# Two more of the 22 gated up-projection blocks computed as seven quarter products, with the shared operands prepared one block earlier

## The chip, the cores and the metric

The kernel runs on one core of one Trainium2 chip. The metric is the time of one execution of the whole program on the device, in microseconds. Tensors are float32. The kernel computes the large matrix products on TensorE with each float32 operand split into a high and a low half of type fp32r; a product of two split operands is three matmuls (high by high, low by high, high by low).

## The reference, cut to what matters

The reference is two transformer-like blocks run one after the other on 512 tokens of 1024 features. The first block mixes stick-breaking attention, a pooling branch and a gated branch, and ends in a feed-forward layer with a squared ReLU. The second block has differential attention and long convolutions, and ends in this gated feed-forward layer, which is where the change sits:

```
def conv_ffn(h, p):
    a, b = jnp.split(h @ p["ffn_w_up"], 2, axis=-1)      # h: 512 x 1024, ffn_w_up: 1024 x 5632
    a = short_conv(a, p["ffn_conv_w"], p["ffn_conv_b"])  # three taps along the tokens
    return (jax.nn.gelu(a, approximate=False) * b) @ p["ffn_w_down"]   # 2816 x 1024
```

The 2816 gate features `a` and the 2816 value features `b` are computed in 22 blocks m = 0 to 21. Block m is 128 gate features and the 128 value features that they multiply, for all 512 tokens.

## The kernel before, in words

All work of an engine stands in one hand-written list per engine, and the lists meet through semaphores: `tensor_program`, `scalar_program` (ACT), `vector_program` (DVE), `gpsimd_program` (POOL) and `sync_program` (SP, which issues most loads). Nothing reorders a list, so an instruction that waits holds back all that stands behind it on its engine.

**Weights.** Weights travel in units of 128x1024 floats (512 KB). SP loads a unit into one of four `raw` buffers (L3122; for the units of the quarter products two halves of 256 KB each, L3118). ACT copies it to a high half `wh` (L1356), and DVE (L2043) or POOL (L2823) subtracts it to make the low half `wl`. There are four slots of `wh`/`wl`. The high copy of unit u waits until TensorE has begun unit u-3 (`w_used`). `weights(x)` in the lists of ACT, DVE, POOL and SP means: do your part for all units up to x.

**Two ways to compute a block.** A plain block (`regular`) is 2 x 8 products of a 128x128 weight with 128x512 of the activations `HTh`/`HTl`: 48 matmuls of 512 columns, from two units of weights. A paired block splits the 1024 input features in two halves, the 512 tokens in two halves, and the features of the block into gate and value. Like Strassen's scheme, it then needs seven quarter products instead of eight. Each is 4 x 3 = 12 matmuls of 256 columns (`product`), so a block has 84 matmuls, from 3.5 units. The weight operands are the four quarters a, b, c, d and the sums ac, cd, acd, abcd. The activation operands are two quarters of `HTh`/`HTl` and five differences of quarters. The differences are shared by all blocks. They are made once: POOL subtracts (`shared_sums`, tile `tf`, L3063), ACT copies the high half (`turned_high`, tile `th`, L1934), DVE subtracts the low half (`turned_low`, tile `tl`, L2718). Their `z` input is the same as that of `HTh`.

The order of the quarter products is `sequence`: cd, acd, d for the first block of a run, then for each later block abcd of the block before, cd, a of the block before, acd, d, b and ac of the block before. Two of them wait for other engines. Product d adds to the PSUM bank in which product cd stands, so it waits until ACT has copied cd out (`keep_cd`, tile `p1c`, L1940). Product abcd waits until DVE has made the difference of acd and that copy (`kernel_sum`, L2724).

**The stages around the change.** Blocks 0 and 1 are plain, with the two halves of the tokens apart (`FIRST`): the first halves during the end of the layer before, the second halves in one stretch after it. In the kernel before, blocks 2 and 3 are plain (`regular`), and blocks 4 to 11 and 12 to 21 are two runs of paired blocks (`RUNS`). After each block the gate goes through ACT's `centre` (L1915), six tap operations on DVE (`up_conv`, L2708), GELU on ACT (`gelu`, L1920), the product with the value on DVE (`up_gate`, L2714), a high copy on ACT (`gated_high`, L1926) and a low half on POOL (`gated_low`, L3052).

**The sums of weights.** They are formed in device memory by DMAs that POOL issues: `sum_weights` copies one quarter and adds another with an accumulating DMA. POOL waits for the DMAs before, since each step needs the result of an earlier one. For the first run, steps 0 to 3 stand in the feed-forward layer of the first block, after that layer's 16th low half (`FFl`, L2969, q = 15), and steps 4 and 5 after its last. Each step moves all blocks of the run. While steps 0 to 3 run, TensorE multiplies by the first half of `w_ff_out`, whose operands need no more from POOL.

## Time and profile before

| What | Value |
|---|---|
| Median of 3 runs | 1447.92 us (1443.75 to 1450.55) |
| The profiled execution's own time | 1448.28 us |
| Its span in the trace | 1446.6 us |
| PE busy | 1429.1 us, 99% of the span |
| DVE, ACT, POOL busy | 60%, 45%, 25% |
| Mean granted clock of TensorE | 0.997 |
| Mean DMA rate | 168 GB/s |

The profiled execution took 1.7 us more than its span (work outside the first and last instruction), and lies 0.4 us above the median of the runs. TensorE's busy share says that it works nearly all the time, but not at which rate. The times of matmuls overlap, so the spacing of their starts is what counts. In the timeline a row is: start in us from the span's start, duration in us, engine, line, operation, output<-inputs, count, and in brackets the idle time before it with what ended it.

### The profile page before, as it was taken

What the parts mean: (1) busy time and instruction counts of PE and PEld (TensorE: products, weight loads), DVE (VectorE), ACT (ScalarE), POOL (GpSimd) and SP (SyncE); (2) the same over time, 40 slices, a digit from 0 to 9 for tenths busy, and PEclk for the clock granted to TensorE, in tenths of its full rate; (3) what the DMA queues carried; (4) which work ended last, traced back from release to release, by engine and by line L of the source; (5) the groups of instructions that cost most, each with busy time, mean ns of one, the idle gap of its engine ahead of it and who ended that gap; (6) DMA issues with size and microseconds to landing.
All of it is one profiled execution on the core that took longest, in us unless ns stands there. A gap on an engine that the chain in (4) does not pass through costs nothing.

```text
span 1446.6 us, 19430 instructions
## 1 busy us (share of the span) xinstructions
PE 1429.1 (99%) x7644; PEld 1206.5 (83%) x7644; DVE 873.9 (60%) x1321; ACT 657.0 (45%) x1048; POOL 366.8 (25%) x315
## 2 busy tenths in 40 slices
PE   9999999999999999999999999999999999999998
PEld 7777778888888888788888888888889899899987
DVE  6455766444477633565438437778757787348854
ACT  6535773233453412334336326665435565236642
POOL 1263211102032200122013422215624142124312
PEclk9999999999999999999999999999999999999999
DMA  8351116654255599656935458854653455345531
GB/s 269 122 170 63 59 44 215 211 167 148 101 200 169 173 292 280 206 182 190 302 109 184 155 188 213 216 198 146 218 160 105 144 177 173 102 130 176 179 128 59
DMA packets 72740, 243.15 MB, mean 168 GB/s; under 512 B 8455, under 2 KB 9384, under 8 KB 67658
## 3 DMA queue, kind: packets, MB, share of 16 engines
q1 hardware_dynamic: 61274, 181.22, 38.3%
q0 software_dynamic: 9744, 55.05, 13.5%
q10 hardware_dynamic: 1632, 5.64, 1.0%
q8 instruction: 61, 1.00, 0.3%
q14 instruction: 29, 0.24, 0.1%
HBM read 229.28 MB, written 50.35 MB: 193 GB/s over the span
## 4 chain that ended last, share of the span: by engine, by line
PE 88%; DVE 4%; DMA 4%; ACT 3%; issue 1%; POOL 0%; SPq 0%; ACTq 0%; DVEq 0%
PE PS L536 86%; DMA raw<-in_ws 3%; PE PS L549 2%; DVE wl L2043 1%; ACT wh L1356 1%; DVE TMP L2708 1%; DVE TMP L2091 0%; DMA X<-in_x 0%; ACT th L1934 0%; ACT HTh L1378 0%; DVE HTl L2059 0%; DVE tl L2718 0%; DVE TMP L2553 0%; DVE TMP L2514 0%; DVE TMP L2714 0%
## 5 line engine op out<-in xcount | busy, mean ns | idle before, releaser
L2043 DVE TENSOR_TENSOR wl<-raw,wh 128x1024 fp32r<-128x1024 f32 x222 | 299.0, 1351 | 302.6 <-ACT wh L1356 302.3
L1356 ACT ACTIVATE wh<-raw 128x1024 fp32r<-128x1024 f32 x255 | 266.7, 1054 | 236.8 <-PE PS L536 144.1
L536 PE MATMUL PS<-HTh,wh 128*128 128x512 f32 (+1 forms) x944 | 348.3, 370 | 3.8 <-DVE wl L2043 2.8
L536 PE MATMUL PS<-HTl,wh 128*128 128x512 f32 (+1 forms) x944 | 345.3, 367 | 0.0
L536 PE MATMUL PS<-HTh,wl 128*128 128x512 f32 (+1 forms) x944 | 341.2, 367 | 0.0
L536 PEld LDWEIGHTS PS<-HTh,wh 128*128 128x128 f32 x944 | 178.7, 189 | 39.3 <-issue 11.4
L536 PEld LDWEIGHTS PS<-HTl,wh 128*128 128x128 f32 x944 | 178.8, 189 | 27.3 <-DVE HTl L2059 0.7
L536 PEld LDWEIGHTS PS<-HTh,wl 128*128 128x128 f32 x944 | 176.4, 189 | 29.5 <-DVE wl L2043 0.2
L536 PE MATMUL PS<-wh,FFh 128*128 128x512 f32 (+1 forms) x442 | 170.0, 385 | 0.1
L536 PE MATMUL PS<-wl,FFh 128*128 128x512 f32 (+1 forms) x442 | 169.9, 384 | 0.0
L536 PE MATMUL PS<-wh,FFl 128*128 128x512 f32 (+1 forms) x442 | 169.8, 384 | 0.0
L2823 POOL TENSOR_TENSOR wl<-raw,wh 128x1024 fp32r<-128x1024 f32 x33 | 82.4, 2499 | 149.7 <-ACT wh L1356 128.8
L536 PE MATMUL PS<-th,wh 128*128 128x256 f32 x360 | 102.6, 285 | 3.3 <-ACT p1c L1940 3.3
L536 PE MATMUL PS<-tl,wh 128*128 128x256 f32 x360 | 102.4, 284 | 0.0
L536 PE MATMUL PS<-th,wl 128*128 128x256 f32 x360 | 102.4, 284 | 0.0
L536 PEld LDWEIGHTS PS<-wh,FFh 128*128 128x128 f32 x442 | 83.1, 188 | 17.0 <-DVE wl L2043 0.5
L536 PEld LDWEIGHTS PS<-wh,FFl 128*128 128x128 f32 x442 | 83.0, 188 | 16.5
L536 PEld LDWEIGHTS PS<-wl,FFh 128*128 128x128 f32 x442 | 83.0, 188 | 16.3
L2969 POOL TENSOR_TENSOR FFl<-TMP,FFh 128x512 fp32r<-128x512 f32 x32 | 43.4, 1355 | 160.1 <-ACT FFh L1591 160.1
L536 PEld LDWEIGHTS PS<-th,wh 128*128 128x128 f32 x360 | 69.6, 193 | 3.6 <-ACT p1c L1940 3.5
L536 PEld LDWEIGHTS PS<-tl,wh 128*128 128x128 f32 x360 | 69.7, 194 | 0.1
L536 PEld LDWEIGHTS PS<-th,wl 128*128 128x128 f32 x360 | 69.7, 194 | 0.0
(359 smaller groups left out, 2328.7 us busy)
## 6 DMA issues: line engine op xcount, KB each, us to landing
raw<-in_ws SPq DMA_DIRECT2D x232, 512.0 KB, 4.6
raw<-sums SPq DMA_DIRECT2D x72, 256.0 KB, 2.9
sums<-in_up POOLq DMA_DIRECT2D x6, 2560.0 KB, 21.1
raw<-in_up SPq DMA_DIRECT2D x54, 256.0 KB, 3.0
sums<-in_up POOLq DMA_DIRECT2D x6, 2048.0 KB, 18.0
sums<-sums POOLq DMA_DIRECT2D x2, 2560.0 KB, 12.9
taps<-TMP SPq DMA_DIRECT2D x16, 256.0 KB, 2.4
tab<-in_spec POOLq DMA_DIRECT2D x8, 512.0 KB, 5.8
```

What stands on the lines that cost most here:

```text
L536: return nc.tensor.matmul(out, l, r, start=start, stop=stop, skip_group_check=True)
L549: return nc.tensor.transpose(out, in_, IDENT)
L1356: act(WH[u % SLOTS][:, :n], RAW[i % RAWS][:, :n], ACT.Copy).then_inc(sem("w_hi"), 1)
L2043: tt(WL[k][:, :n], RAW[RAW_AT["unit", u, 0] % RAWS][:, :n], f32(WH[k][:, :n]), ALU.subtract).then_inc(sem("lo_dve"), 1)
L2708: stt(z[:, do], ps[:, di], pp("ffn_conv_w_2", 22 * w + m), z[:, do], ALU.mult, ALU.add).then_inc(sem("uc_v"), 1)
L2823: tt(WL[k][:, :n], RAW[RAW_AT["unit", u, 0] % RAWS][:, :n], f32(WH[k][:, :n]), ALU.subtract).then_inc(sem("lo_pool"), 1)
L2969: tt(FFl[:, q % 16, :], T(2 + q % 2), f32(FFh[:, q % 16, :]), ALU.subtract).then_inc(sem("ff_lo"), 1)
```

## The change

1. `RUNS` begins with `range(2, 12)`: blocks 2 and 3 are paired blocks, and the first run has ten. Only blocks 0 and 1 stay plain.
2. The high and low halves of the five differences no longer lie beside plain blocks 2 and 3. On ACT, differences 0 and 1 come after `centre(0)`, difference 2 after `centre(1)`, and 3 and 4 after block 1. On DVE, difference 0 comes before `up_gate(0)`, 1 after it, 2 after `up_gate(1)`, 3 after the first `kernel_sum`, and 4 before the first `value_right`.
3. On ACT the weight copy of the fourth unit of the run stands before GELU of block 1, and the first copy of product cd between GELU and the high copy of block 1.
4. `sum_weights` issues one DMA at a time. For the first run each of the eight steps is cut in two pieces of five blocks. Eight pieces stand after the 16th low half of the feed-forward layer, and one after each second low half that follows.
5. The list of units whose low half POOL makes skips the first three units of the second run, as before, whose numbers have moved from 28:31 to 35:38.

```
-RUNS = (range(4, 12), range(12, 22))
+RUNS = (range(2, 12), range(12, 22))
+PIECES = (2, 1)
...
                     centre(m)
+                    for i in ((0, 1), (2,))[m]:
+                        turned_high(i)
+                    if m == 1:
+                        weights(duo_ahead("cd", run[0]))
                     gelu(m)
+                    if m == 1:
+                        keep_cd(run[0])
                     gated_high(m, first_m)
-                    for i in ((0, 1), (2, 3), (4,), ())[m]:
-                        turned_high(i)
-                weights(duo_ahead("cd", run[0]))
-                keep_cd(run[0])
+                if first_m:
+                    weights(duo_ahead("cd", run[0]))
+                    keep_cd(run[0])
+                else:
+                    turned_high(3)
+                    turned_high(4)
...
+                    if m == 0:
+                        turned_low(0)
                     up_gate(m)
-                    for i in ((), (0, 1), (2, 3), (4,))[m]:
-                        turned_low(i)
+                    turned_low(m + 1)
                 weights(duo_ahead("cd", run[0]))
                 kernel_sum(run[0])
+                if first_m == 0:
+                    turned_low(3)
...
+                    if m == RUNS[0][1]:
+                        turned_low(4)
                     value_right(m - 1)
...
+            def sum_weights(n, i, after):
+                f, of, add = (("ac", "c", False), ("cd", "c", False), ("ac", "a", True), ("cd", "d", True),
+                              ("acd", "ac", False), ("acd", "d", True), ("abcd", "acd", False),
+                              ("abcd", "b", True))[i // PIECES[n]]
+                size = len(RUNS[n]) // PIECES[n]
+                at = PAIRED.index(RUNS[n][0]) + i % PIECES[n] * size
+                rows = slice(32 * at, 32 * (at + size))
+                x = a["up4"][PLAIN.index(of), rows, :] if of in PLAIN else a["sums"][SUMMED.index(of), rows, :]
+                y = a["sums"][SUMMED.index(f), rows, :]
+                e.wait_ge("d_sum", 16 * (8 * sum(PIECES[:n]) + after))
...
                 if q == 15:
-                    for step in range(4):
-                        sum_weights(0, step)
+                    for i in range(8):
+                        sum_weights(0, i, i)
+                if q > 15 and q % 2 == 0:
+                    sum_weights(0, q // 2, q // 2)
...
             load_tables(1, 0)
-            sum_weights(0, 4)
-            sum_weights(0, 5)
```

On ACT, from the first weight copy after the second halves of block 0 on, this stood before (L1915 is `centre`, L1920 GELU, L1926 the high copy of the gated block, L1934 the high half of a difference, L1356 a weight copy):

```order
L1356 ACTIVATE wh_72<-raw_68 128x1024 [waits s_w_used,s_d_raw2]
L1915 ACTIVATE TMP_145<-PS,pp_152 128x512 [waits s_p_narrow]
L1920 ACT_TABLE_LOAD
L1920 ACTIVATE TMP_145<-TMP_145 128x512 [waits s_v_narrow]
L1926 ACTIVATE FFh_78<-TMP_145 128x512 [waits s_v_narrow]
L1934 ACTIVATE th_129<-tf_124 128x1024 [waits s_p_wide,s_g_side]
L1934 ACTIVATE th_131<-tf_125 128x1024 [waits s_g_side]
L1356 ACTIVATE wh_73<-raw_69 128x1024 [waits s_w_used,s_d_raw3]
```

In the changed kernel, from `centre(0)` on, this stands there (L1916 is `centre`, L1935 the high half of a difference, L1921 GELU, L1927 the high copy, L1357 a weight copy, L1941 the copy of product cd):

```order
L1916 ACTIVATE TMP_145<-PS,pp_152 128x512 [waits s_p_narrow]
L1935 ACTIVATE th_129<-tf_124 128x1024 [waits s_p_wide,s_g_side]
L1935 ACTIVATE th_131<-tf_125 128x1024 [waits s_g_side]
L1921 ACT_TABLE_LOAD
L1921 ACTIVATE TMP_145<-TMP_145 128x512 [waits s_v_narrow]
L1927 ACTIVATE FFh_78<-TMP_145 128x512 [waits s_v_narrow]
...
L1916 ACTIVATE TMP_145<-PS,pp_152 128x512 [waits s_p_narrow]
L1935 ACTIVATE th_133<-tf_126 128x1024 [waits s_g_side]
L1357 ACTIVATE wh_71<-raw_67 128x1024 [waits s_w_used,s_d_raw1]
L1921 ACTIVATE TMP_145<-TMP_145 128x512 [waits s_v_narrow]
L1941 ACTIVATE p1c_139<-PS 128x256 [waits s_p_score]
L1927 ACTIVATE FFh_78<-TMP_145 128x512 [waits s_v_narrow]
```

Two high halves of differences and the table load now stand between `centre(0)` and GELU of block 0, and the copy of product cd stands behind GELU of block 1, where before it stood behind block 3.

On DVE, this stands in the changed kernel between the taps of block 0 and the first difference of products (L2052 is a low half of weights, L2727 the low half of a difference, L2723 the gate's product, L2717 a tap, L2733 `kernel_sum`; rows of taps left out):

```order
L2052 TENSOR_TENSOR wl_76<-raw_68,wh_72 128x1024 [waits s_w_hi]
L2727 TENSOR_TENSOR tl_130<-tf_124,th_129 128x1024 [waits s_a_exp]
L2723 TENSOR_TENSOR TMP_145<-TMP_145,PS 128x512 [waits s_p_narrow,s_up_g]
L2727 TENSOR_TENSOR tl_132<-tf_125,th_131 128x1024 [waits s_a_exp]
L2052 TENSOR_TENSOR wl_77<-raw_69,wh_73 128x1024 [waits s_w_hi]
L2717 SCALAR_TENSOR_TENSOR TMP_145<-PS,pp_152,TMP_145 128x255 [waits s_v_narrow,s_a_narrow]
...
L2052 TENSOR_TENSOR wl_74<-raw_66,wh_70 128x1024 [waits s_w_hi]
L2723 TENSOR_TENSOR TMP_145<-TMP_145,PS 128x512 [waits s_p_narrow,s_up_g]
L2727 TENSOR_TENSOR tl_134<-tf_126,th_133 128x1024 [waits s_a_exp]
L2052 TENSOR_TENSOR wl_75<-raw_67,wh_71 128x1024 [waits s_w_hi]
L2733 TENSOR_TENSOR p1c_139<-PS,p1c_139 128x256 [waits s_p_score,s_a_filt]
```

Before, no low half of a difference stood before the gate product of block 1. Now one stands ahead of that of block 0, one behind it, and the third ahead of the first `kernel_sum`.

On POOL, around the 16th low half of the feed-forward layer, this stands in the changed kernel (L2978 is the low half, L2864 a copying and L2862 an accumulating DMA; 160 rows are five blocks):

```order
L2978 TENSOR_TENSOR FFl_79<-TMP_145,FFh_78 128x512 [waits s_high] x14
L2864 DMA sums<-in_up 160x2048
L2864 DMA sums<-in_up 160x2048 [waits s_d_sum] x3
L2862 DMA sums<-in_up 160x2048 [waits s_d_sum] x4
L2978 TENSOR_TENSOR FFl_79<-TMP_145,FFh_78 128x512 [waits s_high]
L2864 DMA sums<-sums 160x2048 [waits s_d_sum]
L2978 TENSOR_TENSOR FFl_79<-TMP_145,FFh_78 128x512 [waits s_high] x2
L2864 DMA sums<-sums 160x2048 [waits s_d_sum]
```

Before, six DMAs of 256 rows stood there, the first four in pairs, followed by sixteen low halves with no DMA between them and two DMAs after the last.

## Rows read from the trace of the kernel before

**Rows 1.** The page's first part: busy time of each engine in the whole span.
```profile
PE 1429.1 (99%) x7644; PEld 1206.5 (83%) x7644; DVE 873.9 (60%) x1321; ACT 657.0 (45%) x1048; POOL 366.8 (25%) x315
```
**Rows 2.** Timeline of TensorE: second halves of block 0, of block 1; block 2; first quarter product.
```profile
1103.86 0.28 PE L536 MATMUL PS<-HTh,wh 128*128 128x256 f32 x1
1109.62 0.28 PE L536 MATMUL PS<-HTh,wh 128*128 128x256 f32 x1
1112.14 0.40 PE L536 MATMUL PS<-HTh,wh 128*128 128x512 f32 x1
1133.93 0.28 PE L536 MATMUL PS<-HTh,wh 128*128 128x256 f32 x1
```
**Rows 3.** Timeline of TensorE at the pause before the first product d.
```profile
1136.68 0.28 PE L536 MATMUL PS<-th,wl 128*128 128x256 f32 x1
1140.24 0.58 PE L536 MATMUL PS<-th,wh 128*128 128x256 f32 x1 [3.28 <-ACT p1c L1940]
...
1143.51 0.28 PE L536 MATMUL PS<-HTh,wh 128*128 128x256 f32 x1
```
**Rows 4.** Windows (columns PE, PEld, DVE, ACT, POOL busy, clock, DMA share, GB/s) around the products.
```profile
1140.00:1143.40 3.40, 3.16 (x15) 3.16 (x16) 3.21 (x3) 1.25 (x2) 0.57 (x1) 0.51 0.37 102
1150.00:1200.00 50.00, 50.00 (x419) 50.00 (x418) 40.88 (x69) 30.57 (x43) 15.73 (x9) 1.00 0.60 189
```
**Rows 5.** Timeline of TensorE at the pause in the feed-forward layer of the first block.
```profile
586.05 0.39 PE L536 MATMUL PS<-wh,FFl 128*128 128x512 f32 x1
589.25 0.47 PE L536 MATMUL PS<-HTh,wh 128*128 128x512 f32 x1 [2.81 <-DVE wl L2043]
...
593.89 0.39 PE L536 MATMUL PS<-HTl,wh 128*128 128x512 f32 x1
```
**Rows 6.** The chain of waits before that pause (start us, us, what).
```profile
571.58 15.19 DMA raw<-in_ws
```
**Rows 7.** Timeline of POOL from step 0 of the sums to the last low half.
```profile
504.32 1.13 POOL L2844 DMA_DIRECT2D sums<-in_up  x2
524.82 0.94 POOL L2846 DMA_DIRECT2D sums<-in_up  x1 [19.36 <-DMA sums<-in_up]
...
555.42 0.57 POOL L2849 DMA_DIRECT2D sums<-sums  x1 [28.75 <-DMA sums<-in_up]
568.51 0.88 POOL L2851 DMA_DIRECT2D sums<-in_up  x1 [12.52 <-DMA sums<-sums]
599.01 1.54 POOL L2969 TENSOR_TENSOR FFl<-TMP,FFh 128x512 fp32r<-128x512 f32 x1 [29.63 <-ACT FFh L1591]
...
682.75 1.29 POOL L2969 TENSOR_TENSOR FFl<-TMP,FFh 128x512 fp32r<-128x512 f32 x1 [6.31 <-ACT FFh L1591]
```
**Rows 8.** Timeline of ACT from the second halves of block 0 to product cd's copy.
```profile
1103.88 1.06 ACT L1356 ACTIVATE wh<-raw 128x1024 fp32r<-128x1024 f32 x1 [2.94 <-PE PS L536]
...
1105.63 1.28 ACT L1920 ACT_TABLE_LOAD   x1
1108.23 0.63 ACT L1920 ACTIVATE TMP<-TMP 128x512 f32<-128x512 f32 x1 [1.32 <-DVE TMP L2708]
...
1111.32 1.99 ACT L1934 ACTIVATE th<-tf 128x1024 fp32r<-128x1024 f32 x2
...
1139.83 0.36 ACT L1940 ACTIVATE p1c<-PS 128x256 f32<-128x256 f32 x1
```
**Rows 9.** Timeline of DVE in the same stretch.
```profile
1105.64 2.55 DVE L2708 SCALAR_TENSOR_TENSOR TMP<-PS,pp,TMP 128x255 f32<-128x255 f32 x6 [3.89 <-ACT TMP L1915]
1108.11 2.03 DVE L2043 TENSOR_TENSOR wl<-raw,wh 128x1024 fp32r<-128x1024 f32 x1
...
1119.50 0.68 DVE L2714 TENSOR_TENSOR TMP<-TMP,PS 128x512 f32<-128x512 f32 x1
...
1138.22 1.22 DVE L2718 TENSOR_TENSOR tl<-tf,th 128x1024 fp32r<-128x1024 f32 x1
```
**Rows 10.** Timeline of POOL: the five shared differences.
```profile
1101.93 12.86 POOL L3063 TENSOR_TENSOR tf<-z 128x1024 f32<-128x1024 f32 x5 [0.79 <-DVE HTl L2638]
```

More of the change, by code:

```diff
@@ L191 @@
     or any(u == AT[x][0][0] for x in (((0, 1, 2), 0, 0), ((1, 1, 2), 0, 0), ("w_ff_in", 0, 0)))
-    or u in DUOS and DUOS.index(u) % 7 in (2, 5) and u not in DUOS[:3] + DUOS[28:31])]
+    or u in DUOS and DUOS.index(u) % 7 in (2, 5) and u not in DUOS[:3] + DUOS[35:38])]
 KT = range(8)
@@ L2834, in load_pre @@
                 engine.dma_start(WL[k][:, :], a["wd"][i, 1]).then_inc(sem(f"d_pre{k}"), 16)
-            def sum_weights(n, step):
-                rows = slice(32 * PAIRED.index(RUNS[n][0]), 32 * PAIRED.index(RUNS[n][-1]) + 32)
-                x = {f: a["up4"][i, rows, :] for i, f in enumerate(PLAIN)}
-                y = {f: a["sums"][i, rows, :] for i, f in enumerate(SUMMED)}
-                e.wait_ge("d_sum", 16 * (8 * n + (0, 2, 4, 5, 6, 7)[step]))
-                if step == 0:
-                    for f in ("ac", "cd"):
-                        engine.dma_start(y[f], x["c"], max_dma_last_dim=8192).then_inc(sem("d_sum"), 16)
-                elif step == 1:
-                    engine.dma_start(y["ac"], x["a"], accum_op=ALU.add, max_dma_last_dim=8192).then_inc(sem("d_sum"), 16)
-                    engine.dma_start(y["cd"], x["d"], accum_op=ALU.add, max_dma_last_dim=8192).then_inc(sem("d_sum"), 16)
-                elif step == 2:
-                    engine.dma_start(y["acd"], y["ac"], max_dma_last_dim=8192).then_inc(sem("d_sum"), 16)
-                elif step == 3:
-                    engine.dma_start(y["acd"], x["d"], accum_op=ALU.add, max_dma_last_dim=8192).then_inc(sem("d_sum"), 16)
-                elif step == 4:
-                    engine.dma_start(y["abcd"], y["acd"], max_dma_last_dim=8192).then_inc(sem("d_sum"), 16)
@@ new lines, in sum_weights @@
+            def sum_weights(n, i, after):
[8 more added lines that the diff above has]
+                e.wait_ge("d_sum", 16 * (8 * sum(PIECES[:n]) + after))
+                if add:
+                    engine.dma_start(y, x, accum_op=ALU.add, max_dma_last_dim=8192).then_inc(sem("d_sum"), 16)
@@ L2854, in sum_weights @@
                 else:
-                    engine.dma_start(y["abcd"], x["b"], accum_op=ALU.add, max_dma_last_dim=8192).then_inc(sem("d_sum"), 16)
+                    engine.dma_start(y, x, max_dma_last_dim=8192).then_inc(sem("d_sum"), 16)
             def put_spectrum(o, part):
@@ L3003, in gpsimd_program @@
                 tt(x, x, T(r % 2), ALU.add).then_inc(sem("rp_add"), 1)
-            sum_weights(1, 0)
+            sum_weights(1, 0, 0)
+            sum_weights(1, 1, 0)
             mine = [u for u in range(PRE[2] + 1) if u > unit("w_in_2", 0, 0) and (u in POOL_LOW or u in PRE)]
@@ L3009, in gpsimd_program @@
                 weights(u)
-                if i in (0, 3, 4, 6):
-                    sum_weights(1, (0, 3, 4, 6).index(i) + 1)
+                if i == 0:
+                    sum_weights(1, 2, 2)
+                    sum_weights(1, 3, 2)
+                elif i in (3, 4, 6):
+                    n = 4 + (3, 4, 6).index(i)
+                    sum_weights(1, n, n)
             for o in range(2):
@@ L3029, in gpsimd_program @@
                     weights(unit("w_in_2", 0, 1536 + 10 * P) + SLOTS - 1)
[L3030 removed]
+            sum_weights(1, 7, 7)
             weights(unit("w_out_2", 3 * P, 0) + SLOTS - 1)
```

3 lines of the change are left out of this document (1 added, 2 removed).

## The prediction

> **What bounds the kernel now.** I read the page first: TensorE is busy 99% of the span [rows 1], so what counts is how many matmuls it issues, at which spacing, and where it pauses. The timeline of TensorE gives the spacing. Between the second halves of block 0's value and block 1's value lie 48 matmuls of 256 columns in 5.76 us, 0.120 us each. Blocks 2 and 3 are 96 matmuls of 512 columns from 1112.14 to 1133.93, 0.227 us each [rows 2]. So half the columns cost more than half the time: two matmuls of 256 columns take 0.240.
>
> TensorE pauses for some microseconds in two places that the change touches, and the reader is to see both.
>
> Pause A is in front of the first product d. The last matmul before it starts at 1136.68 and so has its slot until 1136.80; the next starts at 1140.24 and was released by ACT's copy of product cd [rows 3]. That is 3.44 us. Then 15 matmuls take from 1140.24 to 1143.51, 3.27 us where 15 x 0.120 = 1.80 would do. The window there shows a granted clock of 0.51, which is the lower level, 1.2 GHz; before the fall TensorE did nothing for those 3.44 us [rows 4]. So pause A costs 3.44 + 1.47 = 4.91 us.
>
> Pause B is in the feed-forward layer of the first block: from 586.05 + 0.23 to 589.25, 2.97 us, and then 13 matmuls of 512 columns in 4.64 us instead of 2.95 [rows 5]. Together 4.66 us. The chain of waits shows its cause: a load of weights that took 15.19 us and landed at 586.77 [rows 6]. In the same stretch POOL's sums of weights run. The accumulating DMA of step 3 was issued at 568.51, and the chain ends its long load some 18 us later [rows 7].
>
> **The matmuls.** Blocks 2 and 3 lose 48 matmuls of 512 columns each, 48 x 0.227 = 10.90 us, and get 84 of 256 columns, 84 x 0.120 = 10.08. Gain 0.82 per block, **1.6 us** for two. This lies on TensorE's own path in full. The bounds are close: with 50 us / 419 = 0.1193 [rows 4] the gain is 1.8. The Trainium skill, "TensorE: Matmul & The Clock Gate", section "Back-to-back issue gap", gives a spacing of N/2.4 + 2.5 ns at the full clock, 109 and 216 ns here; an estimate by that page is 48 x 0.216 - 84 x 0.109 = 1.2 us per block, 2.4 in all. The trace has 11 ns more for each matmul, and by that the smaller ones lose more; the rows decide.
>
> **The units.** Four units go and seven come. Three more cost ACT 3 x 1.06 us [rows 8] and DVE 3 x 1.22 (the size of a difference's low half, [rows 9]). The steady stretch of paired blocks hides them: from 1150 to 1200 TensorE is busy without a gap, with DVE at 40.88 and ACT at 30.57 of 50 us [rows 4]. Cost nothing; without the cover 3 x 1.2 = 3.7 us. SP's loads for them are of the same bytes per unit. The renumbered list of POOL's units changes nothing in the first run's rhythm, and one unit in seven more or less is covered alike.
>
> **The new start of the products.** Before, blocks 2 and 3 gave the other engines 21.8 us [rows 2] to prepare the differences. Now product cd starts at 1112.14 and runs 12 x 0.120 = 1.44, acd ends at 1115.0, and d needs the copy of cd. I follow the chain of ACT and DVE.
>
> 1. DVE's six taps of block 0 end at 1108.1. The low half of the next unit takes until 1110.1; it lasted 2.03 us against 1.22 for one of its size later on [rows 9], and POOL was busy with the differences just then, from 1101.93 for 12.86 us [rows 10]. The Trainium skill, "GPSIMD Engine Reference", section "Specifications", says that the two share their SBUF interfaces when VectorE has two SBUF inputs; the trace agrees with this.
> 2. The low half of difference 0 now follows. Alone it takes 1.22, beside POOL up to 2.03. I take 2.0, since POOL is busy until 1114.8: 1112.1. The gate's product, 0.6: 1112.7. ACT's table load of 1.28 and two high halves of 1.0 each [rows 8] come before that and are hidden: 1105.6 + 2.0 + 1.3 = 1108.9, and GELU ends by 1109.6.
> 3. ACT: high copy of block 0, 0.55, two weight copies of 1.0, `centre` of block 1, 0.7: 1115.9. DVE meanwhile makes the low halves of difference 1 and of a unit, until about 1116.
> 4. DVE's taps of block 1, 2.5: 1118.4. ACT's difference 2 and one weight copy end at 1117.9, in their cover.
> 5. GELU of block 1, 0.6: 1119.0. Then the copy of cd, 0.36 [rows 8]: **1119.4**.
>
> So TensorE pauses from 1115.0 to 1119.4, 4.4 us, and the clock falls as in rows 3 and 4: 1.5 us more. Product d at the lower clock ends near 1122.1. Product abcd needs the first `kernel_sum`, and DVE has ahead of it, from 1118.4, a low half of weights 1.2, gate product 0.6, low half of difference 2, 1.2, another of weights 1.2, and the subtraction itself, between 0.36 and 0.68, taken as 0.4: 1123.0. **A second pause of 0.9 us.** After it I find nothing late: differences 3 and 4 are due at products b and ac of block 2, near 1130, and are made by 1127.5. Sum: 4.4 + 1.5 + 0.9 = 6.8 us against pause A's 4.91, **1.9 us more**. Bounds: with the low half at 1.22 the chain is 0.8 shorter; with all DVE operations until 1114.8 at 2.03 and POOL's differences later in turn, 1 us longer. So 1.1 to 2.9.
>
> **The sums.** Steps 0 to 3 before: two copies of 2.0 MB together 20.5 us, two accumulations 30.6, one copy 13.1 [rows 7]. A fixed part f and a part x by size: 2x + f = 20.5 and x + f = 13.1 give 7.4 and 5.7 for a copy; for an accumulation, with the same f, x = 12.45. A piece now is 1.25 MB, so a copy 4.6 + 5.7 = 10.3, an accumulation 7.8 + 5.7 = 13.5 us. Bounds: in proportion to size (0.625 of the pairs' halves) 6.4 and 9.6; not shrinking at all 13.1 and 15.3. POOL stands until seven have landed: 4 x 10.3 + 3 x 13.5 = 82 us, from 504.3 to 586, before the next low half is due at 599.0 [rows 7]. It costs TensorE nothing by itself.
>
> What it does for pause B: the stretch moved 6 x 2.0 MB before and moves 8 x 1.25 = 10 MB now, never two DMAs at once, and with f between any two, in which the loads of weights have the DMA engines alone. I take it that the long load no longer comes late and pause B goes: **4.7 us gained**. Bounds: 0 and 4.66.
>
> The other eight pieces stand in the second half of that layer, one after each second low half. Two low halves are 2 x 83.74 / 15 = 11.2 us apart [rows 7]. A copy of 10.3 fits, an accumulation of 13.5 makes POOL's next low half 2.3 late, twice running 4.7. Its input buffer is wanted again two low halves (11.2 us) after it was filled, so between nothing and 11.2 us of lateness is free; I take the middle, 6 us. The Trainium skill, "DMA: Bandwidth & Descriptors", section "Anatomy of one DMA — SWDGE (gpsimd) path", gives a fixed part of about 2.0 us; an estimate by it makes the pieces 7.8 and 10.9 us, and they would fit without lateness. The trace shows no DMA of this size, so the rows leave both open. After the layer, steps 4 and 5 no longer stand on POOL; TensorE did not wait there, so nothing comes of it.
>
> **Sum.** -1.6 + 1.9 - 4.7 = -4.4. The profiled execution's 1448.3 becomes 1443.9; it stood 0.4 above the median of the runs, so I forecast **1443.5**.
>
> **Rivals.**
> - *Pause B stays or moves* (0.20). For it: the last accumulation still ends near the end of the stretch, and accumulations are what the loads suffer under. Against it: less data and gaps. Then 1443.5 + 4.7 = 1448.2.
> - *The start costs less than worked out* (0.10), since TensorE meets shorter gaps and the clock does not fall: 6.8 becomes 3 or less, 1439.5.
> - *The start costs more* (0.08): the copy of cd comes 3 us later, through POOL's late differences or late loads of the summed units: 1446 to 1449.
> - *POOL becomes the pacer of the feed-forward layer; this ends slower* (0.10). If the mean piece takes over (8 x 11.2 + 6) / 8 = 11.9 us, which is just what my two numbers average to, low halves reach TensorE's buffers late. At a mean of 13 the lateness is 8 x 1.8 - 6 = 8 us, plus the clock's 1.5: 1453. At 14.2, the unshrunk bound, 8 x 3.0 - 6 = 18: 1463. For it: rows 7's waits. Against it: f is inferred from contended pairs, and POOL was idle for 6.31 us before the last low half [rows 7].
>
> **How the numbers follow.** My case has 0.52. About 0.5%, 7.2 us, is what a measurement here can tell from no change; the runs before span 6.8. Faster by more needs less than 1440.7: most of the third case, 0.08. Slower by more needs over 1455.1: half of the last, 0.06. Within 0.5% is the rest, 0.86. The range, from 1440 to 1451, leaves out part of the third case and most of the last.
>
> **What would show it.** In the new profile: 84 matmuls per block at 0.120 us for blocks 2 and 3. A pause of 4.4 us released by ACT's `p1c` some 7 us after the second halves end, then a clock of 0.5, then one of 0.9 released by DVE's `p1c`. No pause near 586. Pieces of 10 and 13 us, POOL back before its low half near 599, and no wait of TensorE or ACT for a low half until 690. I am wrong if the pause before d is under 3 us, if the load before 589 still takes 15 us, or if POOL's low halves after 600 are started by a DMA and TensorE waits behind them.

## The result, and the profile after

The changed kernel takes **1455.78 us** (median of 20 runs, 1450.33 to 1457.67) against 1449.62 us for the kernel before (20 runs, 1443.75 to 1453.28). The ratio is 1.0044 with a 95% interval of 1.0032 to 1.0055. So it is slower by 6.2 us, within 0.5% of no change, and the time lies above the range that I gave (1440 to 1451).

The forecast of 1443.5 stood on the median of three runs of the kernel before, 1447.92; the median of 20 is 1449.62, so 1.7 us of the distance of 12.3 us lie in that base.

The profiled execution of the changed kernel took 1450.33 us, which is the lowest of its 20 runs. The first experiment below is the same kernel profiled once more, at a usual time. First the page of the changed kernel, to be read beside [rows 1]:

```profile
PE 1426.4 (98%) x7716; PEld 1207.7 (83%) x7716; DVE 881.4 (61%) x1330; ACT 662.3 (46%) x1055; POOL 377.5 (26%) x325
```

The 72 added matmuls are 2 x (84 - 48), as counted. TensorE's waits, longest first (engine, tile and line waited for: us in total, times, longest):

```profile
PE PS L537 <- ACT p1c L1941: 7.2, 1, 7.2
PE PS L537 <- DVE wl L2052: 1.8, 1, 1.8
PE PS L537 <- DVE p1c L2733: 1.6, 1, 1.6
```

Pause A, 3.28 us [rows 3], has become 7.2 us with another of 1.6 behind it. Pause B, 2.81 us [rows 5], is gone, but there is a new wait of 1.8 us for a low half of weights, later in the same layer.

**The start of the products.** Timeline of TensorE (start us, us, engine, line, operation, idle time before it):

```profile
1112.60 0.28 PE L537 MATMUL PS<-th,wl 128*128 128x256 f32 x1
1120.12 0.58 PE L537 MATMUL PS<-th,wh 128*128 128x256 f32 x1 [7.24 <-ACT p1c L1941]
...
1122.63 0.41 PE L537 MATMUL PS<-th,wl 128*128 128x256 f32 x1
1124.61 0.39 PE L537 MATMUL PS<-HTh,wh 128*128 128x256 f32 x1 [1.56 <-DVE p1c L2733]
```

The windows of the same stretch (columns as in [rows 4]) show the clock at half, 1.2 GHz, while product d runs, after TensorE had done nothing for 7.4 us. The last row is the steady stretch:

```profile
1120.00:1123.40 3.40, 2.93 (x12) 2.63 (x12) 3.40 (x4) 2.57 (x5) 1.54 (x1) 0.50 0.46 154
...
1150.00:1200.00 50.00, 50.00 (x419) 50.00 (x418) 42.12 (x70) 30.52 (x43) 16.32 (x10) 1.00 0.59 184
```

The cost, worked out as for pause A: from 1112.72 (1112.60 + 0.12) to 1120.12, 7.40 us. Product d's 12 matmuls run from 1120.12 to 1122.84, 2.72 us where 12 x 0.120 = 1.44 would do: 1.28. Then nothing until 1124.61, 1.77, and 0.10 on the first matmul after (0.22 us to the next start in place of 0.12). Together 10.55 us against 4.91 before: **+5.6**, where I had +1.9.

A second measure needs no count of pauses: from the first tap of block 0 on DVE to the start of the last copy of cd on ACT the kernel before takes 267.2 us (1105.64 to 1372.82) and the changed one 271.3 (1103.28 to 1374.53). That is 4.1 more, and -1.6 + 5.6 is 4.0. DVE in that stretch says why:

```profile
1103.28 2.55 DVE L2717 SCALAR_TENSOR_TENSOR TMP<-PS,pp,TMP 128x255 f32<-128x255 f32 x6 [3.89 <-ACT TMP L1916]
1105.74 2.03 DVE L2052 TENSOR_TENSOR wl<-raw,wh 128x1024 fp32r<-128x1024 f32 x1
1107.70 3.42 DVE L2727 TENSOR_TENSOR tl<-tf,th 128x1024 fp32r<-128x1024 f32 x1
...
1111.64 2.82 DVE L2727 TENSOR_TENSOR tl<-tf,th 128x1024 fp32r<-128x1024 f32 x1
1114.38 2.28 DVE L2052 TENSOR_TENSOR wl<-raw,wh 128x1024 fp32r<-128x1024 f32 x1
...
1120.77 1.22 DVE L2727 TENSOR_TENSOR tl<-tf,th 128x1024 fp32r<-128x1024 f32 x1
1121.91 2.31 DVE L2052 TENSOR_TENSOR wl<-raw,wh 128x1024 fp32r<-128x1024 f32 x1
1124.14 0.41 DVE L2733 TENSOR_TENSOR p1c<-PS,p1c 128x256 f32<-128x256 f32 x1
```

The low halves of differences 0 and 1 took 3.42 and 2.82 us, the third, of the same shape, 1.22. POOL was making the shared differences beside the first two, and was slower itself than in [rows 10]:

```profile
1099.56 13.82 POOL L3077 TENSOR_TENSOR tf<-z 128x1024 f32<-128x1024 f32 x5 [0.79 <-DVE HTl L2647]
```

The low half of weights at 1121.91 took 2.31 us beside a low half of a gated block on POOL (1121.60, 1.54 us). It stands ahead of `kernel_sum`, which ends the second pause.

ACT stood behind DVE twice on the way to the copy of cd:

```profile
1111.75 0.63 ACT L1927 ACTIVATE FFh<-TMP 128x512 fp32r<-128x512 f32 x1 [4.38 <-DVE TMP L2723]
...
1119.16 0.63 ACT L1921 ACTIVATE TMP<-TMP 128x512 f32<-128x512 f32 x1 [2.33 <-DVE TMP L2717]
1119.70 0.36 ACT L1941 ACTIVATE p1c<-PS 128x256 f32<-128x256 f32 x1
```

**The sums.** Timeline of POOL, pieces of the first and the second half of the layer:

```profile
512.01 0.53 POOL L2864 DMA_DIRECT2D sums<-in_up  x1 [6.96 <-DMA sums<-in_up]
...
549.21 0.84 POOL L2862 DMA_DIRECT2D sums<-in_up  x1 [12.20 <-DMA sums<-in_up]
...
575.16 0.82 POOL L2862 DMA_DIRECT2D sums<-in_up  x1 [12.05 <-DMA sums<-in_up]
593.78 1.54 POOL L2978 TENSOR_TENSOR FFl<-TMP,FFh 128x512 fp32r<-128x512 f32 x1 [17.80 <-ACT FFh L1592]
...
643.10 0.57 POOL L2864 DMA_DIRECT2D sums<-sums  x1 [4.26 <-DMA sums<-in_up]
...
663.12 0.85 POOL L2862 DMA_DIRECT2D sums<-in_up  x1
...
681.25 0.83 POOL L2862 DMA_DIRECT2D sums<-in_up  x1 [5.93 <-DMA sums<-in_up]
685.56 1.29 POOL L2978 TENSOR_TENSOR FFl<-TMP,FFh 128x512 fp32r<-128x512 f32 x1 [3.48 <-ACT FFh L1592]
```

In the first half of the layer a copy takes 7.1 to 8.9 us from issue to issue and an accumulation 13.0 (two in 575.16 - 549.21). In the second half two accumulations took longer: 14.2 us (628.89 to 643.10) and 18.1 (663.12 to 681.25). POOL waits for ACT before every low half, also behind the late pieces, so POOL holds nobody up. The chain of waits from 660 to 700 us does not pass through POOL's low halves but through loads. One of them has 1 KB (`crow`); ACT waits for it ahead of a weight copy, and the `raw` buffer that this frees late is then filled by the load of 10.65 us:

```profile
669.60 11.85 DMA crow<-smallring
...
684.24 10.65 DMA raw<-in_ws
```

The accumulation before the last (663.12 to 681.25) ran beside the 1 KB, the last one, issued at 681.25, beside the load of weights. Windows of both halves of the layer:

```profile
500.00:600.00 100.00, 100.00 (x443) 82.81 (x442) 47.36 (x61) 25.89 (x30) 8.80 (x11) 1.00 0.88 264
600.00:700.00 100.00, 98.05 (x432) 80.54 (x431) 48.37 (x65) 38.48 (x56) 26.12 (x24) 1.00 0.91 268
```

### The profile page after: what moved, and what is told of

Its sections match the earlier page's. It is cut to its first block, busy times and chain, and to the rows that moved or that the text cites. A ratio compares the mean times of both kernels' runs of the same rounds, so it can differ in the third digit from the quotient of the medians.

```text
span 1448.4 us, 19620 instructions
## 1 busy us (share of the span) xinstructions
PE 1426.4 (98%) x7716; PEld 1207.7 (83%) x7716; DVE 881.4 (61%) x1330; ACT 662.3 (46%) x1055; POOL 377.5 (26%) x325
## 4 chain that ended last, share of the span: by engine, by line
PE 88%; DVE 5%; DMA 4%; ACT 2%; issue 1%; POOL 0%; SPq 0%; ACTq 0%; DVEq 0%; POOLq 0%
PE PS L537 85%; DMA raw<-in_ws 3%; PE PS L550 3%; DVE wl L2052 1%; DMA crow<-smallring 1%; ACT wh L1357 1%; DVE TMP L2100 0%; DVE tl L2727 0%; DVE raw L2040 0%; DVE TMP L2717 0%; ACT HTh L1379 0%; DVE HTl L2068 0%; DVE TMP L2562 0%; DVE TMP L2523 0%; POOL wl L2837 0%
## 5 line engine op out<-in xcount | busy, mean ns | idle before, releaser
L2052 DVE TENSOR_TENSOR wl<-raw,wh 128x1024 fp32r<-128x1024 f32 x223 | 302.2, 1358 | 300.0 <-ACT wh L1357 297.2
L1357 ACT ACTIVATE wh<-raw 128x1024 fp32r<-128x1024 f32 x258 | 270.0, 1054 | 231.1 <-PE PS L537 187.6
L537 PE MATMUL PS<-HTh,wh 128*128 128x512 f32 (+1 forms) x928 | 339.6, 367 | 2.5 <-DVE p1c L2733 1.6
L537 PE MATMUL PS<-HTl,wh 128*128 128x512 f32 (+1 forms) x928 | 336.7, 364 | 0.0
L537 PE MATMUL PS<-HTh,wl 128*128 128x512 f32 (+1 forms) x928 | 332.6, 364 | 0.0
L2837 POOL TENSOR_TENSOR wl<-raw,wh 128x1024 fp32r<-128x1024 f32 x35 | 87.6, 2506 | 152.9 <-ACT wh L1357 131.9
L537 PE MATMUL PS<-th,wh 128*128 128x256 f32 x400 | 113.9, 285 | 7.2 <-ACT p1c L1941 7.2
L537 PE MATMUL PS<-tl,wh 128*128 128x256 f32 x400 | 113.7, 284 | 0.0
L537 PE MATMUL PS<-th,wl 128*128 128x256 f32 x400 | 113.7, 284 | 0.0
L537 PEld LDWEIGHTS PS<-th,wh 128*128 128x128 f32 x400 | 77.3, 193 | 7.5 <-ACT p1c L1941 7.4
L2978 POOL TENSOR_TENSOR FFl<-TMP,FFh 128x512 fp32r<-128x512 f32 x32 | 43.3, 1355 | 139.9 <-ACT FFh L1592 139.9
L537 PEld LDWEIGHTS PS<-tl,wh 128*128 128x128 f32 x400 | 77.3, 193 | 0.1
L537 PEld LDWEIGHTS PS<-th,wl 128*128 128x128 f32 x400 | 77.3, 193 | 0.0
```

The costliest lines, as they stand in the source:

```text
L537: return nc.tensor.matmul(out, l, r, start=start, stop=stop, skip_group_check=True)
L1357: act(WH[u % SLOTS][:, :n], RAW[i % RAWS][:, :n], ACT.Copy).then_inc(sem("w_hi"), 1)
L2052: tt(WL[k][:, :n], RAW[RAW_AT["unit", u, 0] % RAWS][:, :n], f32(WH[k][:, :n]), ALU.subtract).then_inc(sem("lo_dve"), 1)
L2837: tt(WL[k][:, :n], RAW[RAW_AT["unit", u, 0] % RAWS][:, :n], f32(WH[k][:, :n]), ALU.subtract).then_inc(sem("lo_pool"), 1)
L2978: tt(FFl[:, q % 16, :], T(2 + q % 2), f32(FFh[:, q % 16, :]), ALU.subtract).then_inc(sem("ff_lo"), 1)
```

## The experiments

The kernels were run in four series, each beside runs of the kernel before on the same chip (median 1449.69 for a, b, c and d; 1450.59 for e, f, g and h; 1449.22 for i and j; 1448.62 for k).

**a. The changed kernel once more.** No edit.

> The changed kernel once more, unchanged. Its first profiled execution (1450.3 us) was one of the fastest of its runs (median 1455.8), so some 5 us of a usual run do not show in that profile. Theory Start (the loss is the longer pauses at the first quarter products, which hang on fixed instruction times): the profile looks as before, 7.2 + 1.6 us of pauses there, and the time stays near 1450. Theory Pieces (the eight pieces of sums that now run beside the second half of the first feed-forward layer delay loads of weights, by an amount that differs from run to run): a profiled execution near 1455 shows waits of TensorE for a weight load of 3 to 7 us between 600 and 700 us, with the start pauses unchanged.

Measured: 1454.64 us (1450.11 to 1457.45, 12 runs), ratio 1.0037 [1.0022, 1.0052]. The profiled execution took 1453.12. The pauses of 7.2 and 1.6 us are the same; the late wait is longer, and the clock falls behind it (timeline of TensorE; two windows):

```profile
692.93 0.80 PE L537 MATMUL PS<-wh,FFh 128*128 128x512 f32 x1 [3.63 <-DVE wl L2052]
```
```profile
600.00:680.00 80.00, 80.00 (x354) 66.24 (x354) 39.35 (x52) 31.16 (x45) 22.86 (x21) 1.00 0.93 278
680.00:700.00 20.00, 16.37 (x67) 13.12 (x66) 9.37 (x14) 7.23 (x10) 3.20 (x4) 0.91 0.84 236
```

67 matmuls from 680 to 700, where the kernel before and the kernels without the wait have 90: 23 x 0.227 = 5.2 us lost. In the first profile it was 79, so 2.5. The chain shows two small transfers of ACT's queue, and DVE standing for the second:

```profile
668.35 12.02 DMA crow<-smallring
...
680.39 11.19 DMA crow<-crow
```
```profile
691.65 1.22 DVE L2052 TENSOR_TENSOR wl<-raw,wh 128x1024 fp32r<-128x1024 f32 x1 [7.92 <-DMA crow<-crow]
```

The first ran beside the accumulation issued at 661.49, which took about 18 us. The second, a broadcast of 128 KB, ran beside the last one, issued at 679.93. In the kernel before the two took 7.9 and 2.9 us. DVE's list waits for `crow` ahead of a low half of weights that TensorE needs. So the late wait has two forms: in the first profile the broadcast took 5.6 us and the wait came through the load of weights, here it came through the broadcast. The theory of the pieces held.

**b. The changed kernel with the old sums.** Six DMAs again (now of 2.5 MB), quarter products as changed.

```
-PIECES = (2, 1)
+PIECES = (1, 1)
...
-                    for i in range(8):
-                        sum_weights(0, i, i)
-                if q > 15 and q % 2 == 0:
-                    sum_weights(0, q // 2, q // 2)
+                    for step in range(4):
+                        sum_weights(0, step)
```

> The changed kernel with the sums of weights issued as before: six DMAs of 2.5 MB after the 16th low half, two after the last, none between. Theory Start: the loss stays, ratio to before about 1.003 to 1.005, since 4 us of start pauses stay and pause B of 4.7 comes back in place of what the pieces cost. Theory Pieces: the waits between 600 and 700 us go and pause B near 586 returns, probably longer than 4.7 us since each step moves a quarter more; time 1451 to 1454, lower than that of the changed kernel by 2 to 4.

Measured: 1456.13 us (7 runs), ratio 1.0047 [1.0030, 1.0064], profiled at 1456.29. The late wait is gone and pause B is back, larger: 4.0 us, with 414 matmuls from 500 to 600 us against 443.

```profile
500.00:600.00 100.00, 96.03 (x414) 78.96 (x413) 37.67 (x49) 20.29 (x23) 5.83 (x7) 0.97 0.98 291
600.00:700.00 100.00, 100.00 (x443) 82.81 (x442) 60.30 (x80) 43.81 (x64) 23.45 (x19) 1.00 0.66 218
```

The signs that the second theory named came, but not its time: 29 matmuls fewer are 29 x 0.227 = 6.6 us lost at pause B, where 4.7 had been lost. So ten blocks make the sums costlier in either form, and the pieces move the loss to the other half of the layer.

**c. The kernel before with the pieces alone.** Blocks 2 and 3 plain, as before; pieces of four blocks, 1.0 MB.

```
+PIECES = (2, 1)
...
-                    for step in range(4):
-                        sum_weights(0, step)
+                    for i in range(8):
+                        sum_weights(0, i, i)
+                if q > 15 and q % 2 == 0:
+                    sum_weights(0, q // 2, q // 2)
```

> The kernel before with only the sums changed: sixteen pieces of 1 MB (four blocks) in the places of the change. Theory Start: the pieces are a gain by themselves (pause B goes), ratio to before 0.997, about 1445. Theory Pieces: ratio to before 1.000 to 1.003, with pause B gone and waits between 600 and 700 us in its place, smaller than in the changed kernel since each piece is a fifth smaller.

Measured: **1443.78** us (1441.66 to 1445.00, 10 runs), ratio 0.9959 [0.9946, 0.9972]. No wait in either half of the layer (443 matmuls in each), and pause A stands as before with 3.3 us. The last accumulation was issued 9.4 us earlier than in the changed kernel, without a wait of POOL. The broadcast of `crow` ran beside it here too and took 11.4 us, and DVE stood for it, but it had been issued at 675.8, 4.6 us earlier than in a, and TensorE did not wait:

```profile
671.81 0.82 POOL L2849 DMA_DIRECT2D sums<-in_up  x1
```
```profile
687.27 1.23 DVE L2044 TENSOR_TENSOR wl<-raw,wh 128x1024 fp32r<-128x1024 f32 x1 [8.08 <-DMA crow<-crow]
```

This is the term of pause B (4.7 us) by itself, and somewhat more: 5.9.

**d. The copy of cd ahead of GELU.** In the changed kernel, directly behind `centre(1)` on ACT.

```
                     centre(m)
+                    if m == 1:
+                        keep_cd(run[0])
...
                     gelu(m)
-                    if m == 1:
-                        keep_cd(run[0])
```

> The changed kernel with ACT's copy of the first product cd directly behind centre of block 1, ahead of difference 2, a weight copy and GELU. Product d should then start when the low half of its weights is made, 3 to 4 us earlier (pause of about 4 us in place of 7.2). If the copy alone sets the end (one theory), the time falls by 3 us. If DVE's kernel_sum, which stands behind two low halves, a gate product and a difference, is as late as it was (the other), product abcd takes over the wait, 4 to 5 us in place of 1.6, and the time stays within 0.5 us.

Measured: 1453.22 us (11 runs), ratio 1.0035 [1.0021, 1.0048]; against the changed kernel's 1454.64 in the same series 1.4 less. The wait for ACT is gone and DVE's are there in its place:

```profile
1116.46 0.36 PE L537 MATMUL PS<-th,wh 128*128 128x256 f32 x1 [3.91 <-DVE wl L2052]
1124.28 0.58 PE L537 MATMUL PS<-HTh,wh 128*128 128x256 f32 x1 [5.33 <-DVE p1c L2733]
```

3.9 + 5.3 = 9.2 us of pauses where there were 8.8. DVE's own times are unchanged (3.42 and 2.83 for the two low halves), and `kernel_sum` starts at 1123.82, where it had started at 1124.14. ACT alone was not the bound, as the second theory had it.

**e. The last four pieces behind the layer.** Pieces 12 to 15 come after its last low half.

```
-                if q > 15 and q % 2 == 0:
+                if q in (16, 18, 20, 22):
...
+            for i in range(12, 16):
+                sum_weights(0, i, i)
```

> The changed kernel with the last four pieces of the sums (all blocks' abcd) behind the feed-forward layer's last low half, one after the other; the first twelve stand where they stood. Known so far: pieces of 1.0 MB alone gave 1443.8 us with no wait between 600 and 700 us, pieces of 1.25 MB give waits of 2 to 4 us there plus a lower clock. Theory Amount (the traffic of the sums in that stretch is what the loads of weights cannot bear): no wait of TensorE between 600 and 700 us, time 1443.8 + 4 to 5 for the start = 1448 to 1449. Theory Start alone (what is lost beyond the start's 4 us belongs to the start in the usual run, where the clock falls for longer): the time stays at 1453 to 1455.

Measured: 1449.85 us (1447.04 to 1450.33, 11 runs), ratio 0.9994 [0.9980, 1.0009]. Some 5 us below the changed kernel, no wait in the layer, the start of the products with 7.2 and 1.6 as before. The four pieces run beside the next stage, from 679.20 to after 714 us, without a wait there. The signs of the first theory came, but k shows that the amount is not the cause.

**f. POOL's later differences wait.** POOL makes the third difference only when DVE has finished two low halves, so that it doesn't work beside them.

```
+                    if t is TF[2]:
+                        e.wait_ge("t_lo", 2)
```

> The changed kernel in which POOL, after the first two shared differences, waits until DVE has made their low halves, and only then subtracts the other three. If DVE's low halves of 3.42 and 2.82 us are long because POOL works beside them, they take 1.2 each, the copy of cd comes near 1116 in place of 1120, the pause before product d is 3 to 4 us in place of 7.2 and the time falls by 3 to 4 us (1451). If they are long for another reason (the table load, the type of the output), they stay as long and the time rises by up to 3, since POOL's differences come later.

Measured: 1454.88 us (12 runs), ratio 1.0023 [1.0011, 1.0036]. DVE and POOL:

```profile
1110.76 1.22 DVE L2727 TENSOR_TENSOR tl<-tf,th 128x1024 fp32r<-128x1024 f32 x1
...
1112.50 1.22 DVE L2727 TENSOR_TENSOR tl<-tf,th 128x1024 fp32r<-128x1024 f32 x1
1114.23 3.05 DVE L2052 TENSOR_TENSOR wl<-raw,wh 128x1024 fp32r<-128x1024 f32 x1 [0.52 <-ACT wh L1357]
...
1119.66 3.23 DVE L2052 TENSOR_TENSOR wl<-raw,wh 128x1024 fp32r<-128x1024 f32 x1
```
```profile
1103.45 4.77 POOL L3079 TENSOR_TENSOR tf<-z 128x1024 f32<-128x1024 f32 x2 [0.79 <-DVE HTl L2647]
1113.80 8.03 POOL L3079 TENSOR_TENSOR tf<-z 128x1024 f32<-128x1024 f32 x3 [5.58 <-DVE tl L2727]
```

The two low halves fall from 3.42 and 2.82 to 1.22 each, and the pause before d from 7.2 to 4.0 us. That is near the pause that the prediction had (4.4). The time that was expected (1451) did not come: POOL's three later differences now lie beside two low halves of weights, which rise to 3.05 and 3.23, and the second pause becomes 4.9. The cause of the long low halves is shown; the remedy only shifts them.

**g. The halves' sum early as well.** As d, and `kernel_sum` on DVE ahead of the taps of block 1.

> As d_copy_early (no gain by itself: product abcd took over the wait, 5.3 us for DVE's kernel_sum), and now kernel_sum stands ahead of block 1's taps on DVE. Product d starts near 1117 and abcd without a wait; a2 or acd3 may wait up to 1.2 us for DVE. The pauses at the start are then 4 + 1 us in place of 7.2 + 1.6, and the time falls by about 4 us against the changed kernel: 1451. If the order of these two were not the cause, nothing would change.

Measured: 1454.95 us (12 runs), ratio 1.0025 [1.0009, 1.0042]. Pauses of 3.89, 0.38 and 3.09 us in front of three products, the last for an addition of DVE (L2752) on which TensorE had not waited at the start before. The expected 1451 was missed:

```profile
1134.81 0.39 PE L537 MATMUL PS<-th,wh 128*128 128x256 f32 x1 [3.09 <-DVE PS L2752]
```

**h. e, f and g together.**

> All three edits together: last four pieces behind the layer, POOL waits for DVE's low halves, cd's copy and kernel_sum early. The pause before d should be under 1 us and the pauses at the start 2 to 3 us in all, no wait between 600 and 700 us: 1440 to 1442, less than the kernel before by 0.5 to 0.7% and less than the pieces alone (1443.8) by 2 to 3 us. If the seven products' own gain of 1.6 us is not there, it ends at 1443 to 1444.

Measured: 1448.26 us (11 runs), ratio 0.9979 [0.9970, 0.9989]. Pauses of 0.67, 2.60 and 3.63 us, 6.9 in all, in front of three different products:

```profile
1127.78 0.58 PE L537 MATMUL PS<-th,wh 128*128 128x256 f32 x1 [3.63 <-DVE PS L2752]
```

The best kernel with blocks 2 and 3 as quarter products, and still slower than c: ratio 0.9979 against 0.9959, or 3.6 us when each is set against the kernel before in its own series. The 1440 to 1442 expected were missed by 6 us or more. The reason is that the sum of the pauses is not the cost. From the first tap of block 0 to the last copy of cd, the stretch measured above, h takes 272.2 us, d 272.5, f 272.4 and g 272.0, where the changed kernel takes 271.3 in both its profiles. With the start left as changed, e and k take 272.9 and 273.5 there, so no new order stands clear of this scatter, and most of what h has gained comes from the pieces, as in e. After the third pause of h the clock is at its lower level once more: TensorE issued 22 matmuls from 1128 to 1132 us, where the steady stretch has 33 in 4 us.

**i. The pieces, and the copy ahead of GELU where the blocks are plain.** c, with three things moved forward in block 3, the last plain one: the copy of cd and a weight copy on ACT, ahead of GELU, and `kernel_sum` on DVE, ahead of the gate product.

```
                     centre(m)
+                    if m == 3:
+                        keep_cd(run[0])
+                        weights(duo_ahead("cd", run[0]))
...
+                    if m == 3:
+                        kernel_sum(run[0])
                     up_gate(m)
```

> The products of blocks 2 and 3 stay as they were, the sums go in pieces of four blocks, and in the last plain block ScalarE makes cd's copy (and the low part of it) ahead of that block's GELU, VectorE the halves' sum ahead of its gate. Theory (the first copy is worth its place when the two plain blocks are not shortened and GpSimd's differences do not lie beside it): pause A, 3.3 us and about 1.5 us of half clock behind it, goes; d's weights are there at about 1134 and the sum at about 1138, just when abcd is due; 1439 to 1440, ratio to before 0.993, 4 us under the kernel with the pieces alone. Rival (VectorE is the bound at the start in any order): the wait moves to abcd or to a low half of weights and is 2 to 4 us there: 1442 to 1444, no gain over the pieces alone.

Measured: **1439.42** us (1439.21 to 1440.00, 6 runs), ratio 0.9941 [0.9920, 0.9961]. The forecast held. The six runs lie within 0.8 us, those of the kernel before in the same series within 8.1 (1443.29 to 1451.38); what makes the latter vary is not shown. The copy of cd now waits for TensorE and not the other way round. What is left is 0.9 us in front of a product further on:

```profile
1130.96 0.38 ACT L1941 ACTIVATE p1c<-PS 128x256 f32<-128x256 f32 x1 [1.77 <-PE PS L537]
```
```profile
1141.94 0.39 PE L537 MATMUL PS<-th,wh 128*128 128x256 f32 x1 [0.94 <-DVE PS L2748]
```

**j. That move alone**, in the kernel before with its old sums.

> The kernel before with the reordered start alone (cd's copy ahead of the GELU, the halves' sum ahead of the gate); sums as before in six pieces. Theory: pause A goes, pause B stays; 1445 to 1446, ratio 0.997. Rival (the wait only moves): 1448 to 1450, ratio 0.999 to 1.000.

Measured: 1444.98 us (1439.16 to 1449.52, 12 runs), ratio 0.9976 [0.9959, 0.9993]. As expected, pause A is gone and pause B is there, with 3.8 us:

```profile
PE PS L536 <- DVE wl L2047: 3.8, 1, 3.8
```

The two gains add: c has 5.9 and j 4.2 us by the medians, together 10.1; i has 9.8. The stretch from the first tap to the last copy of cd is 263.5 us in both i and j, against 267.2 before.

**k. Only the last piece behind the layer.**

```
-                if q > 15 and q % 2 == 0:
+                if q > 15 and q % 2 == 0 and q < 30:
...
+            for i in range(15, 16):
+                sum_weights(0, i, i)
```

> The changed kernel with only the last of the sixteen pieces moved behind the feed-forward layer; the other seven of the second half keep their places and their size. Theory (a late piece: the accumulation issued at 681 us runs beside the loads of the layer's end, where the kernel with pieces of four blocks has issued its last at 672): the wait at 692 to 697 us goes with it, no wait of TensorE from 600 to 700, 1449.5 to 1450.5, as with four pieces moved. Rival (all of the larger pieces load the engines): part of the wait stays, 1452 to 1454.

Measured: 1449.42 us (1447.84 to 1449.63, 12 runs), ratio 1.0002 [0.9994, 1.0011]. As in the first theory, the whole of the late wait goes with one piece of sixteen, though the share of the DMA engines up to 680 us is what it was (0.93 in a):

```profile
600.00:680.00 80.00, 80.00 (x355) 66.24 (x354) 39.14 (x52) 31.13 (x45) 22.93 (x20) 1.00 0.92 280
680.00:700.00 20.00, 20.00 (x90) 16.57 (x89) 9.86 (x15) 7.22 (x10) 3.33 (x4) 1.00 0.83 230
```

The broadcast of `crow`, with no accumulation beside it, took 3.1 us instead of 11.2; the 1 KB before it still took 10.5. The moved piece is not issued much later, 5 us after its place in the changed kernel (681.25) and 6 us after that in a (679.93), behind the two table loads:

```profile
686.09 0.96 POOL L2862 DMA_DIRECT2D sums<-in_up  x1
```

It landed 14.2 us later, ran beside loads of weights just the same, and cost TensorE nothing. So the loss is neither the volume of the sums nor a late issue by itself: it hangs on one accumulation that begins at 680 to 681 us, when the broadcast and the load after it are about to run. With c, whose broadcast was as slow but began at 675.8, the runs say that a slow small transfer costs only where it is late as well.

## Why the prediction was wrong

**The matmuls, -1.6: right, by its parts.** The changed kernel has 419 matmuls in 50 us in the steady stretch, as before, 0.119 us each, and 84 in place of 48 in each of the two blocks. No experiment has this term by itself; together with the start it is confirmed by the 4.1 us above. The Trainium skill's "TensorE: Matmul & The Clock Gate", section "Back-to-back issue gap", would have given 2.4 us; after as before, the trace has 0.119 to 0.120 us for 256 columns where that rule gives 0.109. The section gives the rule for a matmul by itself, which the prediction left out, and for a stream of weight loads and matmuls about 131 ns at 512 columns; the trace has 0.227 us there, so neither figure holds here.

**Pause B, -4.7: right.** It is gone, and c, with pieces of 1.0 MB and the old blocks, shows the gain by itself. The sizes were less exact: copies of 7.1 to 8.9 us where I had 10.3, accumulations of 13.0 where I had 13.5, and in the second half of the layer up to 18.1, above my bound of 15.3; POOL was through with its seventh wait at 575 and not at 586. I suspect the fixed part f = 5.7, which I had fitted to pairs of DMAs that ran at once, but no run separates it from the part by size. The estimates by the Trainium skill's "DMA: Bandwidth & Descriptors", section "Anatomy of one DMA — SWDGE (gpsimd) path", were 7.8 and 10.9: the copies agree with it, the accumulations don't.

**The start of the products, +1.9: wrong, it is +5.6. This is the first step that failed,** in its point 2: "Alone it takes 1.22, beside POOL up to 2.03. I take 2.0". One row of the trace showed a subtraction beside POOL, 2.03 us [rows 9], and I took it for the upper end. The same shape took 3.42 and 2.82 us there, and 3.05 and 3.23 in f. The low half of difference 0 came 1.3 us later by this, that of difference 1 and the low half of weights behind it another 1.7 together (4.95 us from 1111.64 to 1116.59, where the taps begin; I had 3.3). That is the 3 us by which the copy of cd was late: it ended at 1120.06, DVE's taps of block 0 began at 1103.28 here and at 1105.64 before [rows 9], so that 2.4 us are to be added: 1122.4, where I had 1119.4. The second pause was 1.8 us where I had 0.9, with a low half of weights of 2.31 us ahead of `kernel_sum` for which I had 1.2. The order of the steps and who releases the two pauses were as worked out. f confirms the mechanism: without POOL beside them the two low halves take 1.22 us each, and the pause is 4.0. The Trainium skill's "GPSIMD Engine Reference", section "Specifications", says that the two engines share their SBUF interfaces when VectorE has two SBUF inputs. The trace and f agree; I had used the rule for the direction, and a single row for the size, which the page does not give.

What I missed behind that is which engine sets the start. From the taps of block 0 at 1103.3 to the first sum at 1124.5 DVE is busy with hardly a gap, and d, g and h show that each change of order hands the wait to another of its products: 9.2, 7.4 and 6.9 us of pauses, and by the stretch that begins with the taps of block 0 (272.0 to 272.5 us) none of them is shorter than in the changed kernel (271.3). Two plain blocks before gave the engines 21.8 us for this work. Giving up that cover earned 1.6 us. The clock, too, costs more than my 1.5 in some executions: in k product abcd also started at the lower level, and the stretch from the first copy of cd to the last took 257.1 us where it took 254.8 in the changed kernel, 2.3 more with the same waits.

**The second eight pieces, "between nothing and 11.2 us of lateness is free; I take the middle", cost 0: wrong, 2.5 to 5.2 us. This is the second failed step.** It asked only whether POOL would be late with low halves. In the profiles it held up nobody. The pieces fell behind through their own waits (4.26 and 5.93 us), so the last accumulation was issued at 681, where that of c is issued at 672. It ran beside the broadcast and a load of weights, while the one before it ran beside the 1 KB; ACT and DVE stand for these with weights behind them. I had looked at DMAs for their own duration and at POOL, and for the transfers beside them only at pause B. k takes the whole of it away by moving that one piece, and by 5 to 6 us only.

**The sum.** -1.6 + 5.6 - 4.7 + 2.5 = +1.8; the pair of profiled executions gives 1450.33 - 1448.28 = +2.05. With the 5.2 us of a it is +4.5, measured 1453.12 - 1448.28 = +4.84. The medians differ by 6.2; the remaining 1.4 us of that I can't place from single profiles. The clock is a candidate and not shown: e and k, with the same two pauses, took 272.9 and 273.5 us for the stretch from the first tap to the last copy of cd, the changed kernel 271.3.

**The rivals.** "Pause B stays or moves" came nearest, in its second word, with a mechanism that it didn't name. "The start costs more" had the right direction and the wrong reasons and size. POOL as pacer did not occur; that the measured time lies near the 1453 that it gave is chance. (Half of its 0.10 is 0.05, where the prediction has 0.06.)

Left open: why one subtraction beside POOL takes 2.03 us and another of the same shape 3.42; why the accumulation issued at 663 took 18.1 us and others of its size 13.0; and whether smaller pieces (ten blocks in five) would do without moving the last one, which was not tried.

## What to carry to other kernels

Before plain work is replaced by shorter work, count what other engines get done beside it: 1.6 us less of TensorE uncovered some 20 us of DVE work, and every order tried left 7 to 9 us of pauses. Do not add up the pauses alone: h had 1.9 us less of them than the changed kernel and took 0.9 us longer between the same two points in the profiled executions. Where a duration under contention has one row, take that row as a lower bound and look for a reason why it should not be more. When a background transfer is moved, follow it to its end and list the small waits there: one 1.25 MB accumulation issued at 680 us, just ahead of a broadcast that an engine's list waits for, cost 5 us, and nothing when it was issued at 686. The parts of a change can have opposite signs, so run them apart: two of this one's ideas, the pieces and the earlier copy, give 0.9941 without the third.

## What the runs showed of the hardware that was not expected

- A DVE subtraction of 128x1024 with both inputs in SBUF takes 1.22 us alone and 2.0 to 3.4 us when it lies wholly beside POOL's subtractions; the six taps, which read PSUM, took 2.55 us beside POOL (at 1103.28) and 2.53 without (at 1116.59); POOL's own takes 2.4 us when DVE has no such work (4.77 for two) and 2.7 to 2.8 beside it (8.03 for three, 13.82 for five).
- A 1 KB transfer took 9.6 to 13.4 us beside an accumulating DMA of 1.0 or 1.25 MB (c and g, 12.0 in a) and 5.9 to 7.9 us where no sums were moving (e and the kernel before). A broadcast of 128 KB took 5.6 us in one execution and 11.2 in another of the same kernel beside one of 1.25 MB, and 2.9 to 5.8 us where no sums were moving (the kernel before, k and e).
- With the same two pauses 4.5 us apart, the clock was back at its upper level for the product after the second in one execution (its first matmul 0.39 us, the next 0.22 later) and still at the lower one in another (0.58 us), worth 2.3 us.
